# Gate and up weights of a streamed expert FFN as 4 MB transfers into four ring places

## The reference

```python
def expert_ffn(xb, e, w_gate_up, b_gate_up, w_down, b_down):
    gu = xb @ w_gate_up[e] + b_gate_up[e]          # 1024 x 2048 weights, 8 MB an expert
    gate = jnp.minimum(gu[:, :D_FF], SWIGLU_LIMIT)
    up = jnp.clip(gu[:, D_FF:], -SWIGLU_LIMIT, SWIGLU_LIMIT)
    h = (up + 1.0) * gate * jax.nn.sigmoid(SWIGLU_ALPHA * gate)
    return h @ w_down[e] + b_down[e]               # 1024 x 1024 weights, 4 MB an expert
```

## Time and profile before

| | |
|---|---|
| median of three runs | 1069.54 us (1069.49 to 1070.38) |
| profiled execution | 1070.02 us, its span 1068.3 us |
| PE busy | 1014.8 us, 95% |
| DVE, ACT, POOL busy | 207.2, 129.2, 10.8 us |
| DMA | 418.97 MB, mean 392 GB/s |
| granted clock of TensorE | 0.994 |
| transfers of 2 MB (looped experts) | 112 of gate and up, 56 of down |
| transfers of 1 MB (first body) | 32 of gate and up, 16 of down |

### The profile page before, as it was taken

How to read it: one execution, slowest core, us unless ns; L and a number is a source line. 1 busy time by engine, 2 the same in 40 slices (tenths; PEclk the granted TensorE clock), 3 DMA queues, 4 the chain that set the end, 5 groups by cost and what they waited for, 6 DMA issues and landing times.

```text
span 1068.3 us, 11343 instructions
## 1 busy us (share of the span) xinstructions
PE 1014.8 (95%) x4587; PEld 433.7 (41%) x4587; DVE 207.2 (19%) x445; ACT 129.2 (12%) x200; POOL 10.8 (1%) x31
## 2 busy tenths in 40 slices
PE   9999899999999999999999999999999999999996
PEld 6684544343333434343434343333433333333333
DVE  2134421111111212121212111110112121111013
ACT  2462200100000101010101001000101010010002
POOL 1011000000000000000000000000000000000000
PEclk9999999999999999999999999999999999999999
DMA  9955289989999999999999999999999999999991
GB/s 339 415 220 196 113 330 410 401 358 429 428 427 427 427 430 426 429 430 427 427 428 427 430 427 428 429 428 427 429 427 429 429 427 429 426 428 430 427 429 66
DMA packets 38027, 418.97 MB, mean 392 GB/s; under 512 B 4676, under 2 KB 5208, under 8 KB 10360
## 3 DMA queue, kind: packets, MB, share of 16 engines
q1 hardware_dynamic: 36576, 417.61, 93.2%
q10 hardware_dynamic: 1288, 0.55, 0.2%
q0 software_dynamic: 144, 0.52, 0.1%
HBM read 417.62 MB, written 1.05 MB: 392 GB/s over the span
## 4 chain that ended last, share of the span: by engine, by line
PE 66%; DMA 26%; DVE 4%; ACT 2%; issue 2%; ACTq 0%; DVEq 0%; SPq 0%
PE bank L944 64%; DMA ring<-in_w_gate_up_dram 25%; PE bank L1270 2%; DVE area L842 1%; DVE area L838 1%; DVE area L835 1%; DMA area<-in_norm_g_dram 1%; ACT area L542 0%; PE bank L967 0%; DVE xn L922 0%; ACT area L463 0%; ACT area L461 0%; ACT area L459 0%; DVE area L788 0%; ACT L463 0%
## 5 line engine op out<-in xcount | busy, mean ns | idle before, releaser
L944 PE MATMUL bank<-ring,area 128*64 128x512 f32 (+1 forms) x3088 | 701.6, 598 | 27.2 <-DMA ring<-in_w_gate_up_dram 18.2
L944 PEld LDWEIGHTS bank<-ring,area 128*64 128x64 f32 (+1 forms) x3088 | 223.6, 138 | 472.8 <-issue 423.3
L832 DVE TENSOR_SCALAR area<-bank 128x512 f32<-128x512 f32 x32 | 22.1, 691 | 485.0 <-PE bank L944 485.0
L540 ACT ACTIVATE area<-area 128x512 f32<-128x512 f32 x32 | 20.1, 630 | 520.0 <-DVE area L832 520.0
L944 PE MATMUL bank<-masks,xn 128*128 128x128 f32 x544 | 73.0, 288 | 0.0
L944 PEld LDWEIGHTS bank<-masks,xn 128*128 128x128 f32 x544 | 66.7, 196 | 14.5 <-issue 13.8
L944 PE MATMUL bank<-bias,bsel 4*128 4x512 f32 x128 | 63.6, 614 | 0.0
L847 DVE COPY wide<-bank 64x512 f32<-64x512 f32 x32 | 22.2, 694 | 205.6 <-PE bank L944 205.6
L545 ACT ACTIVATE wide<-bank 64x512 f32<-64x512 f32 x32 | 18.8, 589 | 251.6 <-PE bank L944 251.6
L944 PE MATMUL bank<-area,ring 128*128 128x256 f32 x192 | 42.0, 380 | 0.3 <-DVE area L623 0.3
L944 PEld LDWEIGHTS bank<-area,ring 128*128 128x128 f32 x192 | 36.3, 190 | 5.4 <-DVE area L623 0.6
(11 more groups left out here) (137 smaller groups left out, 286.0 us busy)
## 6 DMA issues: line engine op xcount, KB each, us to landing
ring<-in_w_gate_up_dram SPq DMA_DIRECT2D x112, 2048.0 KB, 31.1
ring<-in_w_down_dram SPq DMA_DIRECT2D x56, 2048.0 KB, 34.6
ring<-in_w_gate_up_dram SPq DMA_DIRECT2D x28, 1024.0 KB, 9.7
ring<-in_w_down_dram SPq DMA_DIRECT2D x14, 1024.0 KB, 9.2
ring<-in_w_in_dram SPq DMA_DIRECT2D x8, 512.0 KB, 10.0
ring<-in_w_in_dram SPq DMA_DIRECT2D x4, 1024.0 KB, 17.5
ring<-in_w_out_dram SPq DMA_DIRECT2D x4, 1024.0 KB, 15.9
area<-in_w_gate_up_dram SPq DMA_DIRECT2D x4, 1024.0 KB, 6.8
```

The costliest lines, as they stand in the source:

```text
L540: a.activation(sig, gatec, ACT.Sigmoid, scale=ALPHA).then_inc(sig_ok, 1)
L832: v.tensor_scalar(gatec, gbank[:], LIMIT, None, ALU.min).then_inc(gc, 1)
L944: return t.matmul(o, l, r, start=start, stop=stop, skip_group_check=True)
```

## The change

Gate and up rows go by four: partition p holds rows 4p to 4p+3 of a block of 512, so that four chunks are one run of 32 KB in each partition and one looped transfer of 4 MB into four neighbouring places. Down weights stay at 2 MB. `PARTS` lists the transfers of a looped expert as (first chunk, chunks). The wait of a looped load becomes 12e + (c+n-1) - 15 for n chunks. `ORDER` is changed so that the place at which the loop begins is a multiple of four. PE's waits go to the semaphore of the transfer's first place. Everything that reads the normed input by `d_step` reads it with step 4.

```diff
--- before.py
+++ after.py
@@ -62,21 +62,33 @@
     PLACES = RING + EXTRA
 
 
-    ORDER = [*range(12, 16), *range(0, 8), *range(RING, PLACES), *range(8, 12)]
+    ORDER = [*range(12, 16), *range(0, 4), RING, RING + 1, *range(4, 8), RING + 2, *range(8, 12)]
     FIRST_PLACES = [ORDER[n % PLACES] for n in range(PER_BODY)]
     NEXT_SLOT = next(p for p in ORDER[PER_BODY % PLACES:] if p < RING)
-    assert PER_BODY % RING == 0 and UP_CHUNKS == 8 and DOWN_CHUNKS == 4
+    assert PER_BODY % RING == 0 and UP_CHUNKS == 8 and DOWN_CHUNKS == 4 and NEXT_SLOT % 4 == 0
+
+
+    PARTS = [(0, 4), (4, 4), (8, 2), (10, 2)]
+    PART_OF = [c & ~3 if c < UP_CHUNKS else c & ~1 for c in range(PER_EXPERT)]
 
     def slot_of(n, first=False):
 
         return FIRST_PLACES[n] if first else (NEXT_SLOT + n) % RING
+
+    STARTS = [slot_of(r * PER_EXPERT + c) for r in range(BODY) for c, _ in PARTS]
+
+    def part_start(n):
+
+        return n - n % PER_EXPERT + PART_OF[n % PER_EXPERT]
 
     def loads_of(n, first):
 
 
         if first:
             return n // PLACES + 1
-        return FIRST_PLACES.count(slot_of(n, first) & ~1) + n // RING + 1
+        n = part_start(n)
+        earlier = [slot_of(m) for m in range(n + 1) if part_start(m) == m]
+        return FIRST_PLACES.count(slot_of(n)) + earlier.count(slot_of(n))
 
     rows = {
         "wgu": w_gate_up.rearrange("l e d f -> (l e d) f"),
@@ -127,7 +139,7 @@
         hidT = part(9728, HALF, 4)
 
         gain_f = extra[0][:, 0:D]
-        g2rows = part(7744, 2 * P)[0:4, :]
+        g2rows = part(7744, 4 * P)[0:2, :]
 
 
         wide = sb("wide", [P, D])
@@ -178,8 +190,8 @@
         G2 = vecT[:, 16:24]
 
         def d_step(src, k):
-            lo = (k // 2) * 2 * P
-            return src[:, lo + k % 2:lo + 2 * P:2]
+            lo = (k // 4) * 4 * P
+            return src[:, lo + k % 4:lo + 4 * P:4]
 
         BG, BU, BY, BM = bank[4], bank[5], bank[6], bank[7]
 
@@ -274,8 +286,8 @@
             def rows_of(e, c, n):
 
                 if c < UP_CHUNKS:
-                    src = rows["wgu"][bass.ds(e * D + (c // 2) * 2 * P, 2 * P), :]
-                    return src.rearrange("(p s) f -> p s f", s=2)[:, c % 2:c % 2 + n, :]
+                    src = rows["wgu"][bass.ds(e * D + (c // 4) * 4 * P, 4 * P), :]
+                    return src.rearrange("(p s) f -> p s f", s=4)[:, c % 4:c % 4 + n, :]
                 c -= UP_CHUNKS
                 src = rows["wd"][bass.ds(e * F + (c // 2) * 4 * P, 4 * P), :]
                 return src.rearrange("(p s) f -> p s f", s=4)[:, 2 * (c % 2):2 * (c % 2) + 2 * n, :]
@@ -321,12 +333,12 @@
 
                 sp.wait_ge(bias_used, e - 1)
                 bias_rows(e, m0 // PER_EXPERT)
-                for c in range(0, PER_EXPERT, 2):
+                for c, n in PARTS:
                     s = slot_of(m0 + c)
 
-                    sp.wait_ge(chunks_used, e * PER_EXPERT + (c + 1) - (RING - 1))
-                    src = rows_of(e, c, 2)
-                    dst = ring[:, s * CHUNK:(s + 2) * CHUNK].rearrange("p (s f) -> p s f", s=src.shape[1])
+                    sp.wait_ge(chunks_used, e * PER_EXPERT + (c + n - 1) - (RING - 1))
+                    src = rows_of(e, c, n)
+                    dst = ring[:, s * CHUNK:(s + n) * CHUNK].rearrange("p (s f) -> p s f", s=src.shape[1])
                     sp.dma_start(dst, src).then_inc(chunk_in[s], 16)
 
             for r in range(BODY):
@@ -414,7 +426,7 @@
                                               (pool_scale, 12, 4))):
                 v = src[0, :, :] if len(src.shape) == 3 else src.rearrange("l (r c) -> (l r) c", c=P)
                 act.dma_start(vecs[lo:lo + n, :], v).then_inc(vecs_in[i], 16)
-            act.dma_start(g2rows, norm2_g.rearrange("l (r c) -> (l r) c", c=2 * P)).then_inc(vecs_in[3], 16)
+            act.dma_start(g2rows, norm2_g.rearrange("l (r c) -> (l r) c", c=4 * P)).then_inc(vecs_in[3], 16)
             act.wait_ge(edge_c, 3)
 
             a.activation(stat[:, 15:16], epsc[:], ACT.Sqrt).then_inc(warm, 1)
@@ -435,8 +447,8 @@
                                  scale=G1[:, 4 + k:5 + k]).then_inc(tr_a, 1)
 
             act.dma_start(wpool[:], w_pool[0].rearrange("g c d -> c g d")).then_inc(wpool_in, 16)
-            act.dma_start(wrouter[:].rearrange("p (c s) e -> p c s e", s=2), w_router[0].rearrange(
-                "(c p s) e -> p c s e", p=P, s=2)).then_inc(
+            act.dma_start(wrouter[:].rearrange("p (c s) e -> p c s e", s=4), w_router[0].rearrange(
+                "(c p s) e -> p c s e", p=P, s=4)).then_inc(
                 wrouter_in, 16)
             act.dma_start(brow[:], b_router.broadcast_to([P, NE])).then_inc(brow_in, 16)
             act.dma_start(wide[0:NE, :], b_down[0]).then_inc(bdown_in, 16)
@@ -955,8 +967,8 @@
                 pe.wait_ge(vecs_in[i], 16)
             pe.wait_ge(consts, 8)
             t.transpose(bank[0][:, 0:16], vecs[:], ident[0:16, 0:16])
-            for s in range(2):
-                m = t.transpose(bank[0][:, 16 + s:24:2], g2rows[:, s::2], ident[0:4, 0:4])
+            for s in range(4):
+                m = t.transpose(bank[0][:, 16 + s:24:4], g2rows[:, s::4], ident[0:2, 0:2])
             m.then_inc(vec_t, 1)
 
             def turn(src, tt, halves=(0, 1), stepped=True):
@@ -1211,8 +1223,9 @@
                 if first:
                     pe.wait_ge(chunk_in[slot], 16 * loads_of(m, True))
                 else:
-                    between = 16 * (PER_BODY // RING)
-                    pe.wait_ge(chunk_in[slot & ~1], i * between + (16 * loads_of(m, False) - between))
+                    at = slot_of(part_start(m))
+                    between = 16 * STARTS.count(at)
+                    pe.wait_ge(chunk_in[at], i * between + (16 * loads_of(m, False) - between))
                 return slot
```

## The result

The changed kernel takes 1099.2 us (median of 4 runs, 1097.8 to 1099.8) against 1069.5 us in the same session; the ratio is 1.0276, 95% interval 1.0259 to 1.0294. The direction was the forecast's, the size was not: 29.7 us instead of 2.7, far outside the range of 1068.7 to 1076.4.

A forecast was written before the change was run, and what follows sets the result against it. PE bounds the early loop, the DMA stream sets the end from expert 17. Span 1068.3 + 3.4 - 4.2 + 3.4 + 0.1 = 1071.0 us, median 1072.2, own range 1070.4 to 1073.5; with rivals 1068.7 to 1076.4.

The forecast's parts named there:

- Small edits: Reads by `d_step` at step 4 instead of 2 cost nothing; two more transposes for `g2rows` add 0.1 us.
- the two delays of 3.4 us: Loop's first load goes out 3.4 us later; PE's work behind the last gate and up landing grows 3.4 us.
- Start of the stream: At the loop's start, the first load waits for count 36 instead of 34 with the queue empty: +3.4 us.
- No second hole: After the loop's first 4 MB the queue never empties again, by a thin margin of 0.8 us.
- Rate: Gate and up transfers in the loop: 56 merged pairs save 0.081 us each, taken as -4.2 us, about 430 GB/s.
- Tail: At the end, the last gate and up landing releases four chunks (7.09 us) instead of two (3.65 us): +3.4 us.
- New order of places: Before the loop, the new `ORDER` holds back four ring loads until 91.4 us; cover 8 us, cost nothing.
- (a): Gate and up stream: larger fixed part, rate reaches the best stretch, 7.7 us back, median 1068.7, no change; chance 0.15.
- (c): Experts 3 to 5: 4 MB grain empties the queue once or twice for 1 us, median 1073.2 to 1074.2; chance 0.12.
- (d): Gate and up stream slows to 421 GB/s, +9.1 us instead of -4.2, median 1085.5; chance 0.04.
- (e): Fewer transfers remove engine idling between them: 1.4 us more, median 1070.8; by 2.0 us a transfer near 965, chance 0.01.
- (b): Gate and up stream: runs of 32 KB give nothing, span 1075.2, median 1076.4; chance 0.12.

## Why the prediction was wrong

The step that failed is the one under "Small edits": "Step 4 instead of 2 in `d_step` costs nothing", on the ground of two groups of transposes. It was worth about 27 us: the changed kernel is 29.7 us slower than the kernel before, and 2.9 with the gather at step 2. Each half of the gather took 4.00 us instead of 2.15, and PE bounds the expert loop, not the stream. The direction came out as forecast, but for another reason and so by luck: the two delays of 3.4 us that the forecast counted cost nothing in the changed kernel, where PE never waits for the stream. Three things went wrong in the step.

It took the price from another operation. `d_step` is read by two things, the transposes of `turn`, 16 instructions, and the gather, 544. The rows compared were transposes. For the rate of 32 KB runs, which no row shows, the forecast took bounds from both sides; here one near-looking comparison was taken as the answer. The transposes read with step 4 in the changed kernel are indeed no slower:

```profile
L979 PEld LDWEIGHTS bank<-ident,xres 128*128 128x128 f32 x16 | 2.3, 208 | 1.4 <-issue 0.9 <-DVE xres L736 0.5
```

208 ns instead of 205. The reading was right for them and did not carry over. It also compared step 4 with step 2 only, though the same view of the kernel before has a group of transposes that read at step 1, those of the first norm's output, at 141 ns:

```profile
L967 PEld LDWEIGHTS bank<-ident,xn 128*128 128x128 f32 x16 | 1.7, 141 | 0.0
```

What else differs between the two groups was not separated, but it was a sign that a step could have a price.

It did not multiply. 544 instructions by an unknown of even 50 ns are 27 us, more than all other terms together. That alone should have made the gather's own group one of the rows and its cost an end of the range.

It did not ask how much PE could bear. PE had 1.6 us an expert in hand against the stream, which the forecast worked out and used for other ends. The gather added 1.85 us an expert, of which 1.55 were left, and the stream with 32 KB runs needed 59.0 us a pair, 1.4 us an expert more than PE's 56.15 a pair. Anything above that on PE changes what bounds the kernel; a rival "PE becomes the bound" with that threshold was missing.

The other steps, read where they can be seen, in the changed kernel with step 2:

- Start of the stream: forecast 219.5 us for the first 4 MB, measured 220.13. Right in size. The 0.6 us over it stand in PE's first expert already: its second four chunks start at 142.91 us in that trace, 0.6 later than the 142.33 before, with a granted clock of 0.72 in 124 to 130 us instead of 1.00.
- No second hole: share 1.00 in 221 to 240 us (at 416 GB/s), 1.01 in 240 to 300 and behind. Right.
- Rate: forecast 4.2 us back, about 430 GB/s; measured 431, and 4.1 us between the landings of 32 KB and 16 KB runs. Right; and it is the run that pays, which the forecast had left together with the transfer. The fit of 2.0 us a transfer that the forecast quotes and sets aside is, in the Trainium skill ("DMA: Bandwidth & Descriptors", "Anatomy of one DMA — SWDGE (gpsimd) path"), one for transfers issued by GpSimd; those here are SP's. The transfers of 4 MB in two runs saved next to nothing by being fewer, so the runs speak against it here as the rows did.
- Tail: forecast 31.1 us behind the last landing at 1039.8; measured 31.2 behind 1039.98. Right as a distance; that it can be had back by cutting the last transfer was wrong, as told above.
- New order of places: PE's first expert matmul at 129.95 us in the changed kernel, not later than before. Hidden, as forecast.
- Sum without the failed step: 1072.2 forecast, 1071.7 measured, or 2.7 and 2.9 us above the kernel before of the same session.

Rivals (a), (c), (d) and (e) did not come about, and with 32 KB runs (b) did not either. Its sum, the two delays with nothing back from the rate, is what the experiment that kept 16 KB runs shows: 1076.4 forecast, 1075.7 measured. One term of rival (a) is slightly off in the forecast: at 434 GB/s 56 transfers save 7.6 us, not 7.7.

## What to carry to other kernels

When a change to a transfer's layout changes the step with which an engine reads, list every reader with its count, and take each one's price from its own group. Multiply the count by what you don't know before you call it small, and compare with the slack of that engine against the bound. If a layout wants a wide step in an operand that is read many times, let whoever writes the operand take the step once.

## What the hardware showed

At a granted clock of 1.00, TensorE's float32 matmuls of 128x128 in the gather kept their pace at steps 1 and 2 (2.05 and 2.15 us for 16), slowed at 3 (3.07) and 4 (4.00), and hardly further at 8 (4.10), for a stationary and, at step 4, for a moving operand (3.91). Its transposes at step 4 were no slower than at step 2 (208 ns a weight load, and 205), while a group of transposes at step 1 had 141 ns. VectorE took 1.28 us for 128x1024 elements read at step 4 in two instructions, instead of 0.75 read in order in one. With a full queue, runs of 8, 16 and 32 KB went at 421, 428 and 431 GB/s, the last with a third of the bytes still in runs of 16 KB, and two runs of 16 KB in one transfer at 428.
